# Routing the first eight experts of a product-key lookup ahead of the rest, and moving the transposes around it

## What is computed

```python
h = h + mixed @ w_mix_out
xn = rmsnorm(h, norm2_g)
qh = (xn @ w_q).reshape(tokens, 8, 2, 128)             # two queries a head
scores = einsum('thpc,hpnc->thpn', qh, sub_keys)       # two lists of 128 scores
s_top, i_top = top_k(scores, 16)
cand = s_top[:, :, 0, :, None] + s_top[:, :, 1, None, :]
c_s, c_pos = top_k(cand.reshape(tokens, 8, 256), 16)   # 16 experts a head
e_idx = i_top[..., 0, :] * 128 + i_top[..., 1, :]      # at c_pos
g = softmax(c_s)
a = gelu(einsum('td,thkd->thk', xn, u[e_idx]))
h = h + einsum('thk,thkd->td', g * a, v[e_idx])
return rmsnorm(h, final_norm_g)
```

## Time and profile before

| | us |
|---|---|
| median of 3 runs | 1753.12 (1752.78 to 1753.40) |
| the profiled execution | 1752.94 |
| its span, first to last instruction | 1751.2 |

### The profile page before, as it was taken

How to read it: one execution, slowest core, us unless ns; L and a number is a source line. 1 busy time by engine, 2 the same in 40 slices (tenths; PEclk the granted TensorE clock), 3 DMA queues, 4 the chain that set the end, 5 groups by cost and what they waited for, 6 DMA issues and landing times.

```text
span 1751.2 us, 21314 instructions
## 1 busy us (share of the span) xinstructions
PE 1613.2 (92%) x8160; PEld 1183.5 (68%) x8160; DVE 1159.2 (66%) x2030; ACT 835.1 (48%) x1555; POOL 379.0 (22%) x374
## 2 busy tenths in 40 slices
PE   7999999999999999999999999799987788778786
PEld 6998998888898899888889998455522232222232
DVE  5757865666665776566675556788676767767654
ACT  4456635333455664533355545454444444444443
POOL 0100001000120000100050102565543444334440
PEclk9999999999999999999999999999999999999999
DMA  7444454555544355455544365999999999999996
GB/s 293 161 144 145 152 209 155 198 185 187 198 166 140 125 183 214 168 193 192 186 151 145 145 217 194 414 421 421 422 421 421 422 421 422 422 421 422 421 421 270
DMA packets 67206, 464.43 MB, mean 265 GB/s; under 512 B 7457, under 2 KB 9633, under 8 KB 11809
## 3 DMA queue, kind: packets, MB, share of 16 engines
q0 software_dynamic: 36864, 268.45, 36.9%
q1 hardware_dynamic: 29952, 194.29, 30.8%
q10 hardware_dynamic: 288, 0.33, 0.1%
HBM read 462.00 MB, written 1.05 MB: 264 GB/s over the span
## 4 chain that ended last, share of the span: by engine, by line
PE 65%; DMA 21%; DVE 6%; issue 4%; ACT 3%; POOL 0%; SPq 0%; POOLq 0%; ACTq 0%
PE acc L579 13%; PE acc L581 13%; PE acc L580 13%; DMA arena<-in_peer_uv,arena 10%; DMA row_w_lo<-in_peer_uv,arena 5%; PE att L604 5%; DMA row_w_hi<-in_peer_uv,arena 4%; PE acc L1718 4%; PE acc L1721 4%; PE acc L604 3%; PE att L605 3%; PE acc L605 1%; DVE w_lo L553 1%; DVE arena L2132 1%; PE att L904 1%
## 5 line engine op out<-in xcount | busy, mean ns | idle before, releaser
L553 DVE TENSOR_TENSOR w_lo<-arena,w_hi 128x2048 fp32r<-128x2048 f32 x171 | 391.7, 2300 | 172.8 <-ACT w_hi L546 172.5
L546 ACT CAST w_hi<-arena 128x2048 fp32r<-128x2048 f32 x175 | 333.6, 1907 | 121.8 <-PE acc L581 100.2
L1840 ACT ACTIVATE arena<-arena 128x1 f32<-128x1 f32 x256 | 51.9, 203 | 322.7 <-DVE arena L2132 139.5
L2132 DVE SCALAR_TENSOR_TENSOR arena<-arena 128x1024 f32<-128x1024 f32 x114 | 139.3, 1223 | 84.9 <-DMA arena<-in_peer_uv,arena 83.1
L579 PE MATMUL acc<-xa,w_hi 128*128 128x256 f32 x672 | 192.9, 287 | 0.0
L580 PE MATMUL acc<-xa,w_lo 128*128 128x256 f32 x672 | 190.8, 284 | 0.0
L581 PE MATMUL acc<-xa,w_hi 128*128 128x256 f32 x672 | 190.7, 284 | 0.0
L1718 PE MATMUL acc<-arena,gate_raw 128*128 128x512 f32 x226 | 128.1, 650 | 46.8 <-ACT gate_raw L1850 46.3
L2326 POOL DMA_INDIRECT arena<-in_peer_uv,arena x114 | 129.6, 1137 | 151.4 <-PE acc L1721 141.1
L604 PE MATMUL att<-xa,w_hi 128*128 128x512 f32 x384 | 136.0, 398 | 0.0
L579 PEld LDWEIGHTS acc<-xa,w_hi 128*128 128x128 f32 x672 | 129.2, 192 | 3.6 <-issue 3.0
(11 more groups left out here) (309 smaller groups left out, 3545.7 us busy)
## 6 DMA issues: line engine op xcount, KB each, us to landing
arena<-in_units SPq DMA_DIRECT2D x175, 1024.0 KB, 4.8
arena<-in_bias SPq DMA_DIRECT2D x1, 2048.0 KB, 9.3
arena<-in_peer_uv,arena POOLq DMA_INDIRECT x114
x_res<-in_x SPq DMA_DIRECT2D x2, 512.0 KB, 6.5
arena<-in_norm_mix_g SPq DMA_DIRECT2D x2, 512.0 KB, 6.9
arena<-in_units SPq DMA_DIRECT2D x2, 512.0 KB, 8.1
arena<-in_norm_mlp_g SPq DMA_DIRECT2D x2, 512.0 KB, 6.6
arena<-in_norm_g SPq DMA_DIRECT2D x2, 512.0 KB, 5.8
```

The costliest lines, as they stand in the source:

```text
L546: nc.scalar.copy(w_hi[:, s, :], raw[HOME[g]]).then_inc(S["hi_ready"], 1)
L553: nc.vector.tensor_tensor(w_lo[:, s, :], raw[HOME[g]], w_hi[:, s, :].bitcast(F32), ALU.subtract).then_inc(S["lo_ready"], 1)
L2132: nc.vector.scalar_tensor_tensor(row, row, 1.0, hn[:, n // SLOTS, :], ALU.mult, ALU.mult, accum_out=dots[:, n:n + 1]).then_inc(S["rows_use ...
```

## The change

- A new step on VectorE, first_experts, takes the eight largest scores of each of head 0's lists for tile 0, sums them 8 x 8, takes the eight best sums and their experts, and counts them as ready. (The eight best sums of 16 x 16 are always among the 8 x 8.) It stands ahead of tile_dve of tile 1. route(0, ...) then starts from the eight it has, and writes only experts 8 to 15 of head 0.
- GpSimd waits for these eight ahead of row 0, and for the whole of head 0 ahead of row 8.
- TensorE transposes tile 0 behind 6 passes of mix 3 for tile 1 (18 of tile 1's passes in both units), not 9. It transposes tile 1 behind all queries of tile 0, the ranking of list 1 between the two halves, and starts tile 1's queries behind that. ScalarE copies list 1's queries ahead of tile 1, its scores behind it.
- VectorE makes the rest of tile 0 in one go, ahead of the last addition of the mixer. GpSimd makes the numbers 0 to 15 ahead of tile 1's norm.

```diff
@@ by_tile
-                        half_t(b, s, xh, xl, t, k0[n_], first[n_], last[n_], range(3))
+                        half_t(b, s, xh, xl, t, k0[n_], first[n_], last[n_], range(2))
+                        if n_ == 1:
+                            earlier(t)
+                        half_t(b, s, xh, xl, t, k0[n_], first[n_], last[n_], range(2, 3))
@@ first_queries
                 rank_half(0)
-                tile_pe(pe, "n2", 1)
                 queries_of(0, 1, range(4, 8))
-                queries_of(1, 0, range(2))
+                tile_pe(pe, "n2", 1, range(4))
                 rank_half(1)
-                queries_of(1, 0, range(2, 8))
+                tile_pe(pe, "n2", 1, range(4, 8))
+                queries_of(1, 0, range(8))
                 queries_of(1, 1, range(8))
@@ second_act
             first_rank(0)
+            first_take(1)
             tile_act(act, xb_hi, "n2", 1)
-            first_take(1)
             first_rank(1)
@@ second_dve
+            def first_experts():
+
+                for i in range(2):
+                    scores_ = rank[0][:, i, :]
+                    dve.wait_ge(S["rank_ready"], at("rank_ready", (0, 0, i)))
+                    nc.vector.max(top_s[:, i, 0:8], scores_).then_inc(S["routed"], mark("routed", ("first8", i)))
...
+                    nc.vector.max_index(top_i[:, i, 0:8], top_s[:, i, 0:8], scores_).then_inc(S["routed"], mark("routed", ("first8_at", i)))
...
+                nc.vector.tensor_copy(f_top, top_i[:, :, 0:8]).then_inc(S["routed"], mark("routed", "f_top"))
+                nc.vector.tensor_tensor(f_cand, top_s[:, 0, 0:8].unsqueeze(2).broadcast_to([P, 8, 8]),
+                                        top_s[:, 1, 0:8].unsqueeze(1).broadcast_to([P, 8, 8]), ALU.add).then_inc(
+                    S["routed"], mark("routed", "f_cand"))
...
+                nc.vector.max(f_best, sums_).then_inc(S["routed"], mark("routed", "f_best"))
...
+                nc.vector.max_index(f_pos, f_best, sums_).then_inc(S["routed"], mark("routed", "f_pos"))
...
+                nc.vector.tensor_scalar(f_pos_i[:, 0, :], f_pos, 3, None, ALU.logical_shift_right).then_inc(
...
+                nc.vector.tensor_scalar(f_pos_i[:, 1, :], f_pos, 7, None, ALU.bitwise_and).then_inc(
...
+                nc.vector.tensor_copy(f_pos_f, f_pos_i).then_inc(S["routed"], mark("routed", "f_pos_f"))
...
+                for i in range(2):
+                    nc.vector.tensor_tensor(f_pick[:, i], f_pos_f[:, i, :].unsqueeze(2).broadcast_to([P, 8, 8]),
+                                            iota16[:, 0:8].unsqueeze(1).broadcast_to([P, 8, 8]), ALU.is_equal).then_inc(
+                        S["routed"], mark("routed", ("f_pick", i)))
+                for i in range(2):
...
+                    nc.vector.tensor_tensor(f_pick[:, i], f_pick[:, i], f_top[:, i, :].unsqueeze(1).broadcast_to([P, 8, 8]),
+                                            ALU.mult).then_inc(S["routed"], mark("routed", ("f_picked", i)))
...
+                nc.vector.tensor_reduce(f_both, f_pick, X, ALU.add).then_inc(S["routed"], mark("routed", "f_both"))
...
+                nc.vector.scalar_tensor_tensor(f_expert, f_both[:, 0, :], float(P_KEYS), f_both[:, 1, :], ALU.mult, ALU.add).then_inc(
...
+                nc.vector.tensor_copy(expert[:, 0:8], f_expert).then_inc(S["expert_ready"], mark("expert_ready", "first"))
@@ route
                 if part == 0 and g == 0:
-                    dve.wait_ge(S["iota"], at("iota", 1))
-                    for i in range(2):
-                        dve.wait_ge(S["rank_ready"], at("rank_ready", (0, 0, i)))
-                        top_first(t, h, halves[i:i + 1])
+                    for values, val, idx, i in halves:
+                        dve.wait_ge(S["routed"], at("routed", ("first8_at", i)))
+                        nc.vector.match_replace(values, val[:, 0:8], values, LOWEST).then_inc(
+                            S["routed"], mark("routed", ("top8_out", (t, h, i))))
...
+                    c, known_ = t * SLOTS + h * P_TOP, 8 if g == 0 else 0
+                    nc.vector.tensor_copy(expert[:, c + known_:c + P_TOP], expert_f[:, known_:P_TOP]).then_inc(
@@ peer_norm
                 norm_dve(dve, "n2", 0, g_peer)
-                tile_dve(dve, xb_hi, xb_lo, "n2", 0, [0])
+                tile_dve(dve, xb_hi, xb_lo, "n2", 0)
                 unit("mix", 3)
                 mix_add(1, 1)
-                tile_dve(dve, xb_hi, xb_lo, "n2", 0, [1])
                 norm_dve(dve, "n2", 1, g_peer)
+                first_experts()
                 tile_dve(dve, xb_hi, xb_lo, "n2", 1)
@@ second_pool
             for n in range(ITEMS):
-                if n % P_TOP == 0:
+                if n == 0:
+                    pool.wait_ge(S["expert_ready"], at("expert_ready", "first"))
+                elif n % P_TOP == 0 or n == 8:
```

More of the change, by code:

```diff
@@ L442, in build @@
         wsum = area("ak", 1280, ALL_HEADS)
+        f_top = area("ak", 1296, 16).rearrange("p (i k) -> p i k", i=2)
+        f_cand = area("ak", 1312, 64).rearrange("p (a b) -> p a b", a=8)
+        f_best, f_pos = area("ak", 1376, 8), area("ak", 1384, 8).bitcast(U32)
+        f_pos_i = area("ak", 1392, 16).bitcast(U32).rearrange("p (i k) -> p i k", i=2)
+        f_pos_f = area("ak", 1408, 16).rearrange("p (i k) -> p i k", i=2)
+        f_pick = area("ak", 1424, 128).rearrange("p (i k a) -> p i k a", i=2, k=8)
+        f_both = area("ak", 1552, 16).rearrange("p (i k) -> p i k", i=2)
+        f_expert = area("ak", 1568, 8)
         ROW = 2 * D
@@ L637, in half_t, with by_tile @@
             return m
-        def by_tile(pe, operands, ua, k0, first, last, tag, between=lambda t: None, normed=None, in_halves=False):
+        def by_tile(pe, operands, ua, k0, first, last, tag, between=lambda t: None, normed=None, in_halves=False,
+                    earlier=lambda t: None):
             for t in range(TT):
@@ L701, in norm_dve, with tile_pe @@
                     S["hn_ready"], mark("hn_ready", (tag, t, b)))
-        def tile_pe(pe, tag, t):
-            for k in range(KT):
+        def tile_pe(pe, tag, t, ks=range(KT)):
+            for k in ks:
                 if k % 4 == 0:
@@ L1734, in second_pe @@
                     by_tile(pe, operands, u, (0, 4), (True, False), (False, True), "mix",
-                            lambda t: tile_pe(pe, "n2", 0) if t == 1 else None)
+                            earlier=lambda t: tile_pe(pe, "n2", 0) if t == 1 else None)
                 else:
@@ L2110, in route @@
                     dve.wait_ge(S["routed"], at("routed", ("expert_f", (t, h))))
-                    c = t * SLOTS + h * P_TOP
-                    nc.vector.tensor_copy(expert[:, c:c + P_TOP], expert_f).then_inc(
+                    c, known_ = t * SLOTS + h * P_TOP, 8 if g == 0 else 0
+                    nc.vector.tensor_copy(expert[:, c + known_:c + P_TOP], expert_f[:, known_:P_TOP]).then_inc(
                         S["expert_ready"], mark("expert_ready", (t, h)))
@@ L2305, in second_pool @@
                         n_ += 1
-            for t in range(TT):
-                norm_pool(pool, "n2", t)
+            norm_pool(pool, "n2", 0)
             nc.gpsimd.iota(iota_i, pattern=[[1, P_TOP]], base=0, channel_multiplier=0).then_inc(S["iota"], mark("iota", 0))
@@ L2310, in second_pool @@
             nc.gpsimd.tensor_copy(iota16, iota_i).then_inc(S["iota"], mark("iota", 1))
+            norm_pool(pool, "n2", 1)
             split_lo_by_pool(pool, at_unit2["pq", 1])
```

16 lines of the change are left out of this document (added).

## The result

The changed kernel takes **1763.84 us** in the median (1762.38 to 1765.6) against 1752.95 for the kernel before on the same chip, a ratio of 1.0063 [1.0049, 1.0076]. It is slower by 10.9 us. The forecast of 1754.3 us and its range up to 1758.0 are missed. The profiled execution, from which all rows here come, took 1765.6 us, its span 1763.9.

A forecast was written before the change was run, and what follows sets the result against it. Bound by the DMA stream of 256 gathered rows at 2.49 us each. Lateness of 5.5 + 1.6 us, less 6.3 slack, plus 0.4 for longer issues, gave +1.2 us: 1754.3 us, range 1750.5 to 1758.0.

The forecast's parts named there:

- Part 2, the iota pieces: Transposes and GpSimd's order: list 1's scores come 0.2 us earlier; iota pieces ahead of the second norm delay nothing.
- Part 4, the clock: TensorE's 5.35 us pause before tile 1's first queries halves the clock for 3.3 us, losing 1.6 us (0 to 2.6).
- Rival (b): Low clock lasts through tile 1's 48 short products, losing 5.4 us instead of 1.6: 1758.1 us; chance 0.12.
- signs named for a wrong forecast: No hole in the DMA rate, clock 0.5 beyond 1089, or row 7's gather issued before 1108 or after 1114.
- The sum, slack: Chain through row 0 to row 7's landing: 6.3 us of slack against 7.1 of lateness, plus 0.4 for longer issues.
- The fall ahead of row 0's products: TensorE's clock drop before row 0's products: the same in both kernels, so it cancels.
- Part 3, the queue: VectorE makes x_lo behind first_experts, so tile 1's first queries and everything behind them come 5.5 us late.
- Part 1, the routing: Short routing on VectorE: 3.55 us from list 1's second maximum, giving indices at about 1084.5 instead of 1089.40.
- 4.9 us of head start: Rows 0 to 4, going to free places, are gathered 4.9 us earlier; all the change can bring.
- Rival (a): Gather stream keeps the whole head start and everything comes 4.9 us earlier: 1748.2 us; chance 0.07.

The follow-up runs named there:

- e2: The changed kernel with 2 extra products of 128x512 ahead of tile 1's transposes and 5 behind them, keeping TensorE busy in both pauses: 1756.82 us.
- e11: e1 with one extra product of 128x512 after every 6 of tile 1's 48 short ones: 1764.05 us in a single execution.
- e1: The changed kernel with GpSimd's iota pieces put back behind tile 1's norm: 1760.24 us.
- e6: e1 with 5 extra products of 128x512 in TensorE's one pause: 1758.04 us; four executions at 1753.98 to 1754.74, six at 1757.9 to 1759.86.
- e5: The changed kernel with only tile_dve of tile 1 moved ahead of first_experts, the iota pieces still ahead of the norm: 1758.3 us.
- e4: e1 with tile_dve of tile 1 moved ahead of first_experts: 1751.6 us.
- e3: The kernel before with only the iota pieces moved ahead of tile 1's norm: 1760.06 us.
- e7: e4 with TensorE's and ScalarE's order for tile 1 as in the kernel before: 1750.54 us.
- e8: e4 with 9 extra products of 128x512 in TensorE's pause ahead of row 0: 1749.75 us.
- e10: e7 with 8 extra products of 128x512 in TensorE's pause ahead of row 0: 1749.81 us.

## Why the prediction was wrong, step by step

In the profiled executions the miss closes: forecast +1.2 us, measured +12.7 (last dot product, against 1753.22), and the difference of 11.5 has three terms.

**Part 2, the iota pieces: 3.2 us.** The step that failed first is the sentence that they "lie in its idle time; nothing is queued behind them that is late". Behind the norm and the iota stood the rest of pq1, and what counted was not whether that was late but whether it was early: without the 0.7 us of iota in front it starts before VectorE's norm and holds it off. List 1's scores leave ScalarE at 1084.05 + 0.27 = 1084.3, not at 1080.9, and the 48 products start at 1088.58, not at 1085.35. (About 1.1 of the 3.2 us are the low clock's, which this first pause had brought on: with the pauses filled, in e2, they start at 1087.42.) The row that warned was in the groups: GpSimd's 5.06 us in the earlier trace rows is 0.5 us longer than the 4.54 that it takes when it comes first, and it overlapped the norm by 0.6. The Trainium skill, "SBUF — State Buffer", section "Who interferes with whom", has the rule: a VectorE instruction with two inputs in that memory contends with a GpSimd instruction that reads it, and the one issued first holds the other up entirely. By that rule the trace agrees, in both directions: 5.67 us for 1.41 on VectorE, 5.06 for 4.54 on GpSimd. I had used the section for the gathers only.

**Part 4, the clock: 5.5 us.** The mechanism was right and its term far too small: 1.6 us, from a low clock of 3.3 us, measured 7.2 from 24 us. The 48 short products took 10.3 us instead of 5.4, and pq1's 48 took 8.1 instead of 5.8. The 3.3 us came from the rows' products of 512 columns; e11 shows that behind such products the clock does come back early, and e1 that behind 128-column products it doesn't. Rival (b) named this mechanism, with a chance of 0.12 and a price of 5.4 us; its argument against, "at full clock they held it at 1.00 until 1093", is refuted by e6, where it fell among such products. It also ended the low clock with them, when it lasted into pq1. And TensorE paused twice; the first pause alone is enough (e5). Nor did it take 4.2 us: the first pause began at 1078.73, and the clock fell 1.4 us later (0.52 on average from 1080 to 1084 puts it at about 1080.15). From the start of the 48 products to row 0's dot product the forecast had 19.35 us and the trace has 1113.40 - 1088.58 = 24.82; the 5.5 us between are, within 0.1, the 7.2 less the 1.6. Two of the signs named for a wrong forecast came: a clock of 0.5 beyond 1089, and row 7's gather (1119.86) after 1114.
The sentence from the Trainium skill, "TensorE: Matmul & The Clock Gate", section "Wait — 56ns, not 53.3ns?", went the wrong way too: 106.7 ns for a product of 128 columns at the low clock; these, each with a load of weights of its own, start 213 ns apart. At the high clock they are 112 apart.

**The sum, slack: 2.8 us.** I had 6.3 us less 0.4 for longer issues. Row 0's dot product was 1113.40 - 1097.58 = 15.8 us late against VectorE's being ready before, and the end 12.7: 3.1 us were absorbed. The other kernels say the same by row 40's dot product: 11.0 us late at row 0 and 7.6 at row 40 in e1, 7.5 and 4.7 in e2, 1.9 late and 1.3 early in e4, so 3.4, 2.8 and 3.2 absorbed. It is 3.3 in e3, 3.7 in e7, 4.2 in e6 and 4.6 in e5, but 5.4 in e8 and 6.2 in e10, the two in which the clock doesn't fall ahead of row 0. So a part of this term is a further step of Part 4, "The fall ahead of row 0's products happens in both kernels and cancels": before, the clock was back 3.3 us after these products had started, after, 5.3 us (1115.83 to 1121.1), so that row 1's ran at 1.2 GHz as well. How large that part is stays open, since the kernels with the low clock differ by 1.8 us among themselves. Row 7's gather followed row 0's dot product by 6.46 us, as forecast (6.29). What failed was to count row 7 alone and take the stream as full behind it. It isn't: rows 7 to 10 were in 1135.02 - 1119.86 = 15.2 us after the issue of row 7, where the forecast had 5.63 + 3 x 2.49 = 13.1. Row 8 is issued 3.0 us after row 7 (1119.86 to 1122.90, at the low clock), where it was 1.7 before, and the refilled stream moves 349 GB/s on average from 1122 to 1133, not 421. TensorE frees a place every 2.43 us and a transfer takes 2.49, so what the ring has lost is hardly won back.

**Part 3, the queue, and Part 1, the routing: right.** first_experts took 1087.93 - 1084.35 = 3.58 us (forecast 3.55) and x_lo waited for it; e4, where it doesn't, is 2.9 us faster than e6's lower group. Rows 5 and 6, forecast for 1099 and 1104.7, were issued at 1105.83 and 1113.76, late with the splits that open their places; both were in before row 7 was issued. The 4.9 us of head start were there when the iota was put back: first gather at 1084.24 in e1, 6.1 us earlier than before, 1.0 of it that trace's offset. Rival (a), all of the head start kept (1748.2), was reached by no kernel; the best is e8 with 1749.75.

By runs, the 10.9 us of the medians are 3.6 for the iota's place (after less e1), 5.7 for the clock (e1 less e6's lower group; 7.0 by after less e2, with the iota ahead), and the remaining 1.6 for the order less its head start. The middle number and the remainder rest on the reading of e6's two groups, the first and the sum don't.

What stays open: why the same program (e6) loses the clock in some executions and not in others, and why the shift of single rows behind row 12 still wanders by 1 to 2 us (in e4 the last dot product is 0.35 us early, row 40's 1.3; in e2 row 12's is 2.8 late, row 40's 4.7), which neither a wait nor a stretch explained.

## What to carry to other kernels

Moving small operations ahead on one engine moves everything behind them as well, and early can be as bad as late: ask which large operation now starts first against its neighbour on a shared port. Price a pause on TensorE by what follows it: with short products behind it, a pause of 2.4 us cost here 17 us of halved clock, more than the pause itself. A head start of a stream is worth only as much as the ring behind it lets through, and slack is to be read for several rows behind the first one, not for that alone.

## What the runs showed of the hardware

- Two VectorE instructions with two inputs in memory each, 1.41 us together, that began 0.07 us behind GpSimd's 4.54 us operation ended 1.2 us after it; begun 0.8 us ahead of it, they took their usual time and GpSimd's grew by 0.5 us.
- Products of 128 columns, each with its own weights: 0.112 us apart at 2.4 GHz, 0.213 at 1.2. Products of 256 columns: 0.12 and 0.213.
- The clock was low for 17.1 us after pauses of 2.40 (e5), 3.16 (e3) and 5.20 us (e1) with short products behind, 23.9 us after the two pauses of the change, 10.2 us where it fell among the short products (e6), and 6.8 us in all with long products among the short ones (e11). It came back 3.0 to 5.2 us after 256-column products had followed the short ones, in five traces of five.
- A gather's issue took 3.29 us in the kernel before, where the split of weights ran beside it, and 1.26 at an otherwise like point after; beside a dot product or a split mostly 1.5 to 2.0.
- After a stop of the stream the first data moved about 2 us after the issue of row 7 began (1119.86; 0 GB/s up to 1122).
